# A long convolution's first stages on quarters of the array, its rows permuted to 4 partitions apart

## What is computed

```
def hyena_filters(L, ...):
    hdn = jnp.sin(freq[1] * (jnp.sin(freq[0] * (feats @ fw1 + fb1)) @ fw2 + fb2))
    h = (hdn @ fw3).reshape(L, HY_ORDER, 2, D_MODEL)
    return h * jnp.exp(-t * jnp.abs(deltas))[:, None, None, :]

def bidir_long_conv(z, h_fwd, h_bwd, bias):
    k = jnp.concatenate([h_fwd, jnp.zeros_like(h_fwd[:1]), h_bwd[1:][::-1]], axis=0)
    y = jnp.fft.irfft(jnp.fft.rfft(z, n=2 * L, axis=1) * jnp.fft.rfft(k, n=2 * L, axis=0), n=2 * L, axis=1)[:, :L]
    return y + z * bias

u = short_conv(h @ w_in + b_in, conv_w, conv_b)
x1, x2, v = jnp.split(u, 3, axis=-1)
z = v
for n, gate in enumerate((x1, x2)):
    z = gate * bidir_long_conv(z, filt[:, n, 0], filt[:, n, 1], fbias[n])
return z @ w_out + b_out
```

## Time and profile before

| | us |
|---|---|
| median of 3 runs | 3582.74 |
| lowest and highest | 3571.73, 3589.32 |
| the profiled execution | 3569.07 |
| its span | 3567.4 |
| PE busy in it | 3304.8 |
| DVE busy | 2143.4 |
| ACT busy | 1313.7 |
| POOL busy | 313.9 |

### The profile page before, as it was taken

How to read it: one execution, slowest core, us unless ns; L and a number is a source line. 1 busy time by engine, 2 the same in 40 slices (tenths; PEclk the granted TensorE clock), 3 DMA queues, 4 the chain that set the end, 5 groups by cost and what they waited for, 6 DMA issues and landing times.

```text
span 3567.4 us, 47950 instructions
## 1 busy us (share of the span) xinstructions
PE 3304.8 (93%) x18338; PEld 2581.6 (72%) x18338; DVE 2143.4 (60%) x3189; ACT 1313.7 (37%) x2216; POOL 313.9 (9%) x510
## 2 busy tenths in 40 slices
PE   7999889999798999999899889999999979999897
PEld 4888545555576888887788757777778758887685
DVE  6998734444466554554767555555556576655676
ACT  3212333343344333333345433333334353333344
POOL 0111234344200000000000200000000000000000
PEclk8999999999898999999999999999999989999899
DMA  7666777897701332224435310000002133333532
GB/s 294 202 200 200 214 137 155 159 170 161 253 29 57 121 95 83 80 83 176 158 97 161 128 49 15 8 7 7 7 25 77 48 110 103 104 107 118 213 98 89
DMA packets 183689, 410.15 MB, mean 115 GB/s; under 512 B 33263, under 2 KB 60207, under 8 KB 180791
## 3 DMA queue, kind: packets, MB, share of 16 engines
q1 hardware_dynamic: 131288, 270.69, 23.1%
q0 software_dynamic: 51936, 131.27, 15.5%
q10 hardware_dynamic: 288, 5.77, 0.4%
HBM read 262.51 MB, written 81.00 MB: 96 GB/s over the span
## 4 chain that ended last, share of the span: by engine, by line
PE 74%; DVE 12%; DMA 7%; ACT 3%; issue 2%; POOL 1%; SPq 1%; DVEq 0%; ACTq 0%
PE ps L624 20%; PE ps L625 19%; PE ps L626 19%; PE ps L2426 3%; PE ps L2360 2%; PE ps L2378 2%; DMA t2z<-s 2%; PE ps L2398 2%; PE ps L694 1%; DVE mx L2798 1%; DMA t2k<-s 1%; PE ps L2269 1%; DMA traw<-hidden_scratch 1%; PE ps L2461 1%; POOL t2z L1962 1%
## 5 line engine op out<-in xcount | busy, mean ns | idle before, releaser
L624 PE MATMUL ps<-HB,gsp 128*128 128x512 f32 x1232 | 489.0, 397 | 37.4 <-DVE HB L800 22.0
L625 PE MATMUL ps<-HB,gsp 128*128 128x512 f32 x1232 | 485.2, 394 | 0.0
L626 PE MATMUL ps<-HB,gsp 128*128 128x512 f32 x1232 | 483.5, 392 | 0.0
L1078 DVE TENSOR_TENSOR gsp<-graw,gsp 128x512 fp32r<-128x512 f32 x330 | 226.4, 690 | 262.4 <-ACT gsp L1057 261.7
L1057 ACT ACTIVATE gsp<-graw 128x512 fp32r<-128x512 f32 x330 | 206.6, 628 | 325.0 <-PE ps L626 266.0
L624 PEld LDWEIGHTS ps<-HB,gsp 128*128 128x128 f32 x1232 | 234.3, 190 | 90.7 <-issue 21.5
L624 PE MATMUL ps<-tsp,wdh 128*128 128x512 f32 x616 | 243.6, 395 | 38.0 <-DVE tsp L1335 37.9
L626 PEld LDWEIGHTS ps<-HB,gsp 128*128 128x128 f32 x1232 | 234.3, 190 | 49.9
L625 PEld LDWEIGHTS ps<-HB,gsp 128*128 128x128 f32 x1232 | 234.8, 191 | 46.3 <-issue 1.0
L626 PE MATMUL ps<-tsp,wdh 128*128 128x512 f32 x616 | 241.9, 393 | 0.0
L625 PE MATMUL ps<-tsp,wdh 128*128 128x512 f32 x616 | 241.8, 393 | 0.0
(11 more groups left out here) (280 smaller groups left out, 7556.6 us busy)
## 6 DMA issues: line engine op xcount, KB each, us to landing
graw<-in_w_gu SPq DMA_DIRECT2D x176, 256.0 KB, 2.7
mring<-in_mod_w POOLq DMA_DIRECT2D x78, 512.0 KB, 4.7
hidden_scratch<-R SPq DMA_DIRECT2D x154, 256.0 KB, 2.4
traw<-hidden_scratch SPq DMA_DIRECT2D x154, 256.0 KB, 2.7
t2k<-s POOLq DMA_DIRECT2D x80, 256.0 KB, 5.9
t2z<-s POOLq DMA_DIRECT2D x160, 128.0 KB, 7.9
t2w<-w POOLq DMA_DIRECT2D x160, 128.0 KB, 5.4
wd<-in_w_dx SPq DMA_DIRECT2D x6, 2816.0 KB, 15.6
```

Of the source, the lines that this page charges most:

```text
L624: pe.matmul(o, wh, xh, start=start, stop=False, skip_group_check=onto)
L625: pe.matmul(o, wh, xl, start=False, stop=False, skip_group_check=onto)
L626: return pe.matmul(o, wl, xh, start=False, stop=stop, skip_group_check=onto)
L1078: dve.tensor_tensor(gsp[U % 3][:, 1, :], graw[:, q, W_SLOT[i], :], gsp[U % 3][:, 0, :].bitcast(F32), ALU.subtract).then_inc(w.lo, 1)
```

## The change

Four things change together, in the convolution alone.

- **Rows.** `dft_constants` permutes the rows of the second-stage matrices (`st`, `f1i`), so that scatters go to other partitions: `landing_row` and `group_row` place a scatter's 8 partitions 4 apart within 32 (NB = 16). For the context `t2k` and `t2z` go to 32 partitions 2 apart in one half, `t2w` stays 4 apart.
- **The filter in pairs.** Two phases, c = 0 and 1, are made at once in quarters: phase c goes to PSUM's half c, and the two directions to the two A banks. `h2` needs its blocks alone. A whole quarter of the filter is one unit for the first stage: it waits for both pairs (`s_ae`, `au + 4`), then two first-stage calls of eight quarter matmuls each follow in the next step. `ksb` has three slots of two.
- **The signal on quarters.** The first stage takes 64 rows and 64 columns of the array at a time, eight calls of 256 columns a unit instead of two of 512.
- **Buffers.** B is a pair of banks used in turn (pairs 4 and 2), `s1` has four slots of 1024 columns, ScalarE copies 1024 at a time, `w1` has seven buffers. S and M wait where they share pairs with B.

```
+def landing_row(NB, h, c, quarter):
+    return 64 * h + (32 * c + quarter if NB == 16 else c)
+def group_row(NB, g):
+    return 64 * (g % 2) + 32 * (g // 2 % 2) + g // 4 if NB == 16 else g
...
+            landed[landing_row(NB, h, c, quarter) + (4 if NB == 16 else 2) * (slots * v + s)] = slot * NB + i
+            gathered[group_row(NB, i) + 4 * slot] = slot * NB + i
+    st, f1i = st[landed], f1i[gathered]
...
-        BANK_A, BANK_B = (0, 1), (2, 3)
-        SETS_C, SETS_D, SETS_S = ((4, 2), (4, 0)), ((6, 0), (6, 2)), (4, 6)
+        BANK_A, SETS_B = (0, 1), (4, 2)
+        SETS_C, SETS_D, SETS_S = ((4, 2), (6, 0)), ((6, 0), (4, 2)), (4, 6)
...
-                        pool.dma_start(by_partition(t2k, it, n2, 0 if it < NCH else 512 * cc, 512), s1[b % 8][:]
+                        for h in range(2):
+                            c = h ^ i
+                            pool.dma_start(landing(t2k, it, h, c, o if it < NCH else 0, 0 if it < NCH else 512 * o, 512),
+                                           s1[b % 4][:, 512 * c:512 * c + 512]).then_inc(s_s1o[b % 4], 16)
...
+                        for c in range(2):
+                            for h in range(2):
+                                pool.dma_start(landing(t2z, it, h, c, u if it < NCH else 0, 0 if it < NCH else CW * u, CW),
+                                               s1[b % 4][:, CW * (2 * h + c):CW * (2 * h + c + 1)]).then_inc(s_s1o[b % 4], 16)
...
-                pe.matmul(bank(BANK_B[b % 2]), f1[:, which, 2, :], ksb[ku % 2][:], start=True, stop=True
+                pe.wait_ge(s_ae, au + 4)
+                bank_b_free(b)
+                for way in range(2):
+                    for r, v in QUARTERS:
+                        mm = pe.matmul(ps[rows64(v), SETS_B[b % 2] + r, :], f1[rows64(r), which, way, rows64(r ^ i)],
+                                       ksb[2 * ((kp + v) % 3) + way][rows64(r), :], start=way == 0, stop=way == 1)
...
+                for h in range(2):
+                    for r, v in QUARTERS:
+                        mm = pe.matmul(ps[rows64(v), SETS_B[b % 2] + r, CW * h:CW * (h + 1)], f1[rows64(r), which, 0, rows64(h)],
+                                       zsb[zu % 2][rows64(r), CW * v:CW * (v + 1)], start=True, stop=True)
...
+                        if au:
+                            pe.wait_ge(s_ae, au)
                         bank_a_free(au)
-                        pe.matmul(bank(BANK_A[au % 2]), h2[:, g0 + n2, :], fw3[kb % 2][:].rearrange("p o c -> p (o c)"),
-                                  start=True, stop=True).then_inc(s_af, 1)
+                        for c, n2 in enumerate((first, second)):
+                            for r in range(2):
+                                mm = pe.matmul(ps[rows64(c), BANK_A[r], :], h2[rows64(r), g0 + n2, :],
+                                               fw3[kb % 2][rows64(r)].rearrange("p o c -> p (o c)"), start=True, stop=True)
+                        forward_held(1)
+                    held += [("K", n["A"], n["B"] + i, 8 * it + 2 * o, which, i) for i in range(2)]
...
+                    pe.wait_ge(s_be, n["B"] - 1)
...
-                        if ku >= 2:
-                            dve.wait_ge(s_bf, KB_AT[ku - 2] + 1)
+                        if ku >= 6:
+                            dve.wait_ge(s_bf, KB_AT[(ku // 2 - 3) // 2 * 2 + 1] + 1)
```

More of the change, by code:

```diff
@@ L112, in dft_constants @@
                 st[:, g, 0, col], st[:, g, 1, col] = vre, vim
+    landed, gathered = np.zeros(P, int), np.zeros(P, int)
+    slots = 64 // NB
+    for slot in range(2 * slots):
+        for i in range(NB):
+            c, rest = divmod(i, NB // 2)
+            quarter, v = divmod(rest, 2)
+            h, s = divmod(slot, slots)
+            landed[landing_row(NB, h, c, quarter) + (4 if NB == 16 else 2) * (slots * v + s)] = slot * NB + i
+            gathered[group_row(NB, i) + 4 * slot] = slot * NB + i
+    st, f1i = st[landed], f1i[gathered]
     half = [slice(32 * r, 32 * r + 32) for r in range(2)]
@@ L137, in filter_constants @@
     nt = -t[m, 0].T
-    return np.ascontiguousarray(ft), np.ascontiguousarray(nt)
+    pairs = np.zeros((P, NB), np.float32)
+    for j in range(NB // 2):
+        for v in range(2):
+            for c in range(2):
+                pairs[64 * c:64 * c + 64, 2 * j + v] = nt[64 * v:64 * v + 64, j + c * NB // 2]
+    return np.ascontiguousarray(ft), pairs
 def constants():
@@ L2068, in _ @@
                     for u in range(4):
-                        n2, cc, kb = filter_unit(it, o, u)
+                        first, second, cc, kb = filter_pair(it, o, u // 2)
                         ku = 16 * it + 4 * o + u
-                        g0 = NBX * series(it)
+                        at = NBX + u if it == NCH else 4 * o + u
                         act.wait_ge(s_jl[kb % 2], 48 * (kb // 2 + 1))
@@ L2074, in _ @@
                             act.wait_ge(s_ae, KA_AT[ku - 2] + 1)
-                        act.activation(dec[ku % 2][:], dlt[kb % 2][:, 0:CW], ACT.Exp,
-                                       scale=nt[:, g0 + n2:g0 + n2 + 1]).then_inc(s_dec, 1)
+                        act.activation(dec[ku % 2][:], dlt[kb % 2][:, 0:CW], ACT.Exp, scale=nt[:, at:at + 1]).then_inc(s_dec, 1)
+                        if u % 2 == 1 and taken < n["B"]:
+                            sent_out(taken)
+                            taken += 1
+                elif kind == "Z":
+                    for u in range(4):
                         for b in range(taken, n["B"] + u):
@@ L2079, in _ @@
                         taken = n["B"] + u
-                elif kind == "Z":
-                    for u in range(4):
-                        for b in range(taken, n["B"] + 2 * u):
-                            sent_out(b)
-                        taken = n["B"] + 2 * u
                 else:
```

203 lines of the change are left out of this document (105 added, 98 removed).

## The result

The changed kernel took **3599.15 us** (median of 5, 3598.72 to 3602.80), the kernel before 3578.01 us beside it (median of 5, 3571.73 to 3589.32): a ratio of **1.0046**, 95% interval 1.0027 to 1.0066. Forecast was 3549 us, in a range of 3512 to 3592. The profiled execution took 3599.0 us where that of before took 3569.1. The whole difference lies in the convolution: it ran from 391.6 to 964.0 us and runs from 391.9 to 999.7 us now, 35 us longer, of which the parts behind it get 5 back. The profiled execution of before lay 9 us under its median, so 35 us of stretches stand beside 21 us of medians.

What follows compares the result with a forecast made beforehand. The prediction took the convolution to be bound mostly by PE's own work, plus waits for `t2z` scatters and the filter's multiplies. Its terms summed to -34 us, from a median of 3582.7 to 3549 us, range 3512 to 3592.

Steps and rivals of the forecast that it cites:

- 391.6 to 470.0: First stretch of the convolution, 78.4 us: 67 us forecast, -11.5, with the 9.5 us `t2z` wait cut to some 3.
- K0 with B: Filter step K0 and B behind it, 15.6 us: 16.6 forecast, +1.0 in each of four iterations.
- K1 with Z: Filter step K1 and the signal's Z, 14.0 us: 14.7 forecast, +0.7 in each of four iterations.
- K2, K3 and M: Last filter steps and M, 33.3 to 36.8 us: 29.7 forecast, 31 in iteration 3, -20 over four iterations.
- Z and S: Signal steps Z and S, 14.2 us: 12.9 forecast, -1.3 in each of four iterations.
- the other waits for `t2z`: PE's other three waits for `t2z` scatters, 10.5 us, mostly before the context's last M: -4 forecast.
- If the scatters keep up: Condition put on the -20 us for the last filter steps and M of the four iterations.
- rival 3: ScalarE's copies wait for `s1` slots, decays queue behind, PE waits: 5 us in each K2-K3, 3606 us; chance 0.12.
- The 1.7 us lie bare once per step: In consecutive filter steps PE waits 1.7 us for VectorE to empty both A banks: 6.8 us a step, no gain.
- rivals 1 and 2: Scatters stay as slow, about 3581 us, chance 0.15; or rise only to 187 GB/s, about 3565 us, chance 0.17.
- costed at nothing: Context's `t2k` and `t2z` rows going from 4 to 2 apart: nothing in the sum, up to +5 us in the range.
- Rival 4: Paper saving of 68 us comes in nearly full, with the 20 us of DMA waits: 3500 us; chance 0.06.

Runs made afterwards that it cites:

- e12: Changed kernel with only the added waits of the filler code and no idle matmuls, as control: 3599.57 us, 1.0036.
- e7: Changed kernel with two idle matmuls of 256 columns in each of two waits of a filter step: 3576.32 us, 0.9984.
- e9: e1 plus idle matmuls of 512 columns in the context, eight in its wait for `t2z`, fourteen ahead of the last B: 3551.52 us, 0.9913.
- e8: e1 with all four of ScalarE's decays of a filter step ahead of the evictions that wait for `s1` slots: 3568.72 us, 0.9956.
- e4: Changed kernel with the long series' rows of `t2k` and `t2z` 8 apart and those of `t2w` 16 apart: 3651.03 us, 1.0192.
- e1: Changed kernel with a filter step's second pair in two idle PSUM banks, 6 and 7: 3560.11 us, 0.9929.
- e3: Changed kernel with the filter in the old order, one unit at a time, its scatters cut in two: 3569.05 us, 0.9967.

## Why the prediction was wrong

Its terms, and what the profile shows (sum over the iterations, us):

| term | predicted | measured |
|---|---|---|
| 391.6 to 470.0 | -11.5 | 78.4 to 77.8: -0.6 |
| K0 with B, x4 | +4.0 | 15.4, 15.6, 16.0, 17.8 to 22.1, 22.0, 21.9, 22.0: +23 |
| K1 with Z, x4 | +2.8 | 14.0, 14.0, 14.1, 14.8 to 16.3, 16.1, 16.0, 18.1: +10 |
| K2, K3 and M, x4 | -20 | 36.7, 33.3, 32.8, 36.8 to 35.0, 35.0, 34.7, 34.6: 0 |
| Z and S, x4 | -5.2 | 14.2 to 13.1: -4.6 |
| the other waits for `t2z` | -4 | from an iteration's last B to K0, summed: -4.6; the context's end 17.6 to 22.3, 26.2 to 27.9, 7.4 to 13.5: +12 |

The terms summed to -34 us and measured +35.

- **The step that failed** is "K0 with B: 16.6" and its neighbour "K1 with Z: 14.7", 26 us of the 69 us between. They were reckoned with durations of PE's matmuls at a granted clock of 1.00, as the earlier trace rows show it for those stretches, in a kernel whose PE hardly stood there. The same sum laid 1.7 to 2.4 us bare waits into every filter step and left the durations behind them as they were. The clock was in the column all along and is in no sentence of the prediction; no rival had it. K0 itself came near (6.7 us for 5.65 and the wait for its last multiply); B behind it was reckoned at 11.0 us and took 15.3. e12 against e7 prices this at 19 us, e9 at 5.7 more in the last B: together more than the 21 us by which the kernel became slower.
- **The largest term, -20 for K2, K3 and M, came to nothing**, and mostly not by the clock: no kernel with the filter in pairs got under 33.5 us, where 29.7 were forecast, e7 with its higher clock neither. M with F behind it came in as reckoned (18.95 us for 18.8), but K2 and K3 took 16.0 us for 10.9:
```profile
625.20:633.70 8.50, 3.03 (x39) 1.16 (x36) 2.58 (x4) 4.17 (x8) 7.38 (x13) 0.88 0.93 255
633.70:641.20 7.50, 7.50 (x48) 2.50 (x52) 1.29 (x2) 2.30 (x4) 1.75 (x4) 0.68 0.68 196
```
"If the scatters keep up" failed: `t2z` landed in 8.0 us there (9.1 before). ScalarE waited 17.5 us for slots, the mechanism of rival 3 (.12), at about 5 us an iteration as said there; its condition was wrong, for it came with a faster queue. The queue of decays that it named holds K2 and K3, but with the queue gone PE waits as long for the scatters at M (e8).
- The first stretch, -11.5: the filter steps ran at a clock of 0.70 until 402.5 us and 0.85 until Z, which began at 427.1 us, no earlier than before (426.5); S waited 4.0 us for Z's scatters, and M took 16.9 us for 15.3 at a clock of 0.86. Only the wait ahead of M shrank as planned, from 9.5 to 4.8 us.
- "The 1.7 us lie bare once per step": it did where filter steps follow each other (steady steps of 6.4 to 6.9 us in the first stretch, 6.8 forecast), and bare waits for `ksb` are 49.0 us in 20. The second pair of banks takes 16 us of PE's waits for `ksb` away and is worth 20 us beside e7. Two signs that the prediction gave of being wrong or right were missed as well: K2 took 8.5 us where 7.5 was the limit, and PE's waits for `t2z` are 24.3 us in sum (15.4 and 8.9), not under 8.
- The scatters: about 300 GB/s assumed, 268 measured over Z and S by the queue's share of engine time, landing 3.8 us. The rate held, and rivals 1 and 2 did not come true. With the engines full and the queue nearly alone the rate is read directly, over 635 to 638 us:
```profile
635.00:638.00 3.00, 3.00 (x17) 0.85 (x13) 1.29 (x2) 0.00 (x0) 0.00 (x0) 0.50 0.99 274
```
- Of 4 ports against 8 (the Trainium skill, SBUF — State Buffer, Door 1) the first half agrees roughly: 122 (before) and 127 GB/s (e4) for `t2w` with rows 16 apart, at shares of 1.10 and 1.08, beside an estimate of 109 by the page; over Z and S, with `t2z` too, it was 155.
- The context "costed at nothing": 224 GB/s instead of 354 made PE's wait 15.4 us where 7.8 stood. The page's 8 ports, some 218 GB/s, would have given this; the prediction has it in a sentence on its own and not in the sum. For 4 apart in one half the same page gives the same 218, and there 274 was measured, so it would have misled there.
- Z and S: right to 0.2 us a time. Of the 68 us that were to leave PE on paper, 17 left its busy time, since matmuls at half clock are busy for longer (e1, with less half-clock time, shows 43), and not one microsecond reached the end.

Rival 4 stayed out of reach, and the forecast sign was wrong: with the clock held up in the filter steps (e7) the change is 0.9984, hardly a difference; it is a gain with the second pair of banks (e1, 0.9929) or with the filter left in its old order (e3, 0.9967).

## What to carry to other kernels

When an edit takes work off TensorE but leaves it waiting, look at the granted clock of the stretches behind the new waits before counting the saving: durations read at 1.00 did not hold here once the engine stood ahead of them. A buffer that one unit filled and two units fill now needs a second copy in the same edit (here two idle PSUM banks turned +0.5% into -0.7%). Where a wait can't be removed, a little unneeded work in it can pay, if it ends before the wait does and matmuls follow at once; it speeds up the work behind the wait, not the wait. And when one wait goes, look at what the next step waits for (here the scatters at M) before counting the gain.

## What the runs showed of the hardware

- Adding two unneeded matmuls per wait made the kernel 19 us faster (e7 against e12); four gave 11.
- A scatter's rate depends on which rows it writes. With the DMA engines full: `t2w` 16 apart 122 and 127 GB/s, 4 apart in one half 274 (changed, 635 to 638 us), `t2z` 2 apart in one half 209 (895 to 900 us). By q0's share of engine time: Z and S 155 with 16 apart and 268 with 4 apart, the context's `t2z` 354 with 4 apart over both halves, 224 with 2 apart and 300 with 4 apart in one half. The context's filter, 256 KB scatters 2 apart, is an outlier: 131 GB/s at a share of 1.04 (870 to 880 us).
- A step in which PE worked 2.97 of 6.7 us, its longest gap 2.9 us, was followed by 6.2 us at half clock.
